# A decoder layer on one core: two of four weight sums of each Strassen unit by an adding transfer

## What is computed

```python
def _half_ffn(x, norm_g, w_gate, w_up, w_down):     # D_FF = 2816
    h = _rmsnorm(x, norm_g)
    return x + 0.5 * ((jax.nn.silu(h @ w_gate) * (h @ w_up)) @ w_down)
...
xp = _half_ffn(xp, ffn1_norm[l], ffn1_w_gate[l], ffn1_w_up[l], ffn1_w_down[l])
u, q, k, v = _project(_rmsnorm(xp, mix_norm[l]), pos_p, w_in[l], q_norm[l], k_norm[l])
mixed = jnp.concatenate([_pool_mix(u, pos_p, pool_w[l], pool_scale[l]),
                         _swa_prompt(q, k, v, attn_sinks[l])], axis=-1)
xp = xp + mixed @ w_out[l]
xp = _half_ffn(xp, ffn2_norm[l], ffn2_w_gate[l], ffn2_w_up[l], ffn2_w_down[l])
```

## Time and profile before

| | |
|---|---|
| median of 3 runs | 894.06 us (893.58 to 895.48) |
| profiled execution | 894.41 us, of which the span is 892.6 us |
| PE busy | 879.5 us (99%) |
| DVE busy | 659.2 us (74%) |
| ACT busy | 393.6 us (44%) |
| POOL busy | 32.4 us (4%) |
| DMA | 98.57 MB, mean 110 GB/s |

### The profile page before, as it was taken

One profiled execution on the slowest core, in us unless ns is written; L12 is line 12 of the kernel. 1 busy time (PEld: TensorE's weight loads), 2 busy tenths in 40 slices (PEclk: granted clock), 3 DMA queues, 4 the chain that ended last, 5 costly groups with the idle time before them and its releaser, 6 DMA issues.

```text
span 892.6 us, 17068 instructions
## 1 busy us (share of the span) xinstructions
PE 879.5 (99%) x7100; PEld 861.9 (97%) x7100; DVE 659.2 (74%) x956; ACT 393.6 (44%) x635; POOL 32.4 (4%) x37
## 2 busy tenths in 40 slices
PE   8999999999999999999988999999999999999998
PEld 7999999999999999999867999999999999999998
DVE  7969556997479976743777588997469984699844
ACT  8635213554135544433455446554125552255520
POOL 0000000000000000013322000000000000000000
PEclk9999999999999999999988999999999999999999
DMA  7233313422333323423201323433424424244241
GB/s 260 102 122 127 131 48 123 144 89 94 131 119 119 119 84 119 158 86 100 95 1 45 124 71 118 125 113 101 148 73 153 130 74 153 78 146 131 80 122 61
DMA packets 43180, 98.57 MB, mean 110 GB/s; under 512 B 4288, under 2 KB 5056, under 8 KB 43104
## 3 DMA queue, kind: packets, MB, share of 16 engines
q1 hardware_dynamic: 41056, 94.67, 32.0%
q10 hardware_dynamic: 2048, 2.81, 0.9%
HBM read 93.53 MB, written 3.60 MB: 109 GB/s over the span
## 4 chain that ended last, share of the span: by engine, by line
PE 93%; DVE 4%; ACT 1%; issue 1%; DMA 0%; POOLq 0%; SPq 0%; POOL 0%; DVEq 0%
PE ps L580 44%; PE ps L709 15%; PE ps L711 15%; PE ps L710 15%; PE ps L611 1%; ACT prob L1337 1%; DVE small L1832 1%; DVE prob L1848 1%; PE ps L768 1%; DMA raw<-gu 0%; DVE small L1836 0%; DVE wlo L1453 0%; PE ps L931 0%; PE ps L850 0%; PE ps L949 0%
## 5 line engine op out<-in xcount | busy, mean ns | idle before, releaser
L709 PE MATMUL ps<-xhi,whi 128*128 128x260 f32 (+1 forms) x1092 | 310.2, 284 | 0.1
L711 PE MATMUL ps<-xhi,wlo 128*128 128x260 f32 (+1 forms) x1092 | 310.0, 284 | 0.0
L710 PE MATMUL ps<-xlo,whi 128*128 128x260 f32 (+1 forms) x1092 | 309.6, 283 | 0.0
L709 PEld LDWEIGHTS ps<-xhi,whi 128*128 128x128 f32 x1092 | 205.4, 188 | 0.8 <-issue 0.6
L711 PEld LDWEIGHTS ps<-xhi,wlo 128*128 128x128 f32 x1092 | 205.5, 188 | 0.0
L710 PEld LDWEIGHTS ps<-xlo,whi 128*128 128x128 f32 x1092 | 205.4, 188 | 0.0
L1524 DVE TENSOR_TENSOR wlo<-full,whi 128x1024 fp32r<-128x1024 f32 (+1 forms) x117 | 160.3, 1394 | 0.0
L1065 ACT CAST whi<-raw 128x1024 fp32r<-128x1024 f32 (+1 forms) x75 | 75.3, 1004 | 178.3 <-PE ps L580 171.3
L580 PE MATMUL ps<-hhi,whi 128*128 128x268 f32 (+1 forms) x690 | 140.4, 285 | 0.3
L580 PE MATMUL ps<-hlo,whi 128*128 128x268 f32 (+1 forms) x690 | 140.1, 284 | 0.0
L580 PE MATMUL ps<-hhi,wlo 128*128 128x268 f32 (+1 forms) x690 | 139.7, 284 | 0.0
(11 more groups left out here) (194 smaller groups left out, 1082.6 us busy)
## 6 DMA issues: line engine op xcount, KB each, us to landing
full<-gu SPq DMA_DIRECT2D x78, 512.0 KB, 4.3
raw<-d SPq DMA_DIRECT2D x32, 448.0 KB, 3.5
full<-gu SPq DMA_DIRECT2D x39, 256.0 KB, 2.7
raw<-d SPq DMA_DIRECT2D x16, 512.0 KB, 3.6
raw<-w_in SPq DMA_DIRECT2D x10, 512.0 KB, 3.7
raw<-gu SPq DMA_DIRECT2D x9, 512.0 KB, 3.6
raw<-w_out SPq DMA_DIRECT2D x8, 512.0 KB, 4.5
xT<-x SPq DMA_DIRECT2D x8, 268.0 KB, 5.6
```

Source lines behind the costliest of these rows:

```text
L709: nc.tensor.matmul(dst, whi_t, xhi_t, start=(first and pr == 0), stop=False, skip_group_check=True)
L710: nc.tensor.matmul(dst, whi_t, xlo_t, start=False, stop=False, skip_group_check=True)
L711: last = nc.tensor.matmul(dst, wlo_t, xhi_t, start=False, stop=(pr == KC - 1), skip_group_check=True)
```

## The change

The first of VectorE's sums (line 1509) is taken out. In its place GpSimd issues a transfer for each unit that reads blocks 0 and 3 from memory once more (512 KB) and adds them to what stands in slots 1 and 4, after it has waited for the load of block 2 into these slots. `added` becomes one semaphore for each of the three buffers, counted up by 16 as the transfer lands; hi_a and the next sum wait for it. The transfers of stage 0 stand at the start of GpSimd's program, those of stage 1 at its end.

```diff
@@ build
-    added = sem("added")
+    added = [sem(f"added{r}") for r in range(3)]
@@ hi_a, on ScalarE
-            act.wait_ge(added, unit_no(s, p, i) + 1)
+            act.wait_ge(added[i % 3], k)
@@ weight_sums, on VectorE
             dve.wait_ge(b_loaded[r], k)
-            dve.wait_ge(c_loaded[r], k)
-            nc.vector.tensor_tensor(full[:, r, 1:5:3, :], full[:, r, 1:5:3, :], full[:, r, 0:7:6, :], ALU.add
-                                    ).then_inc(added, 1)
-            dve.wait_ge(added, u + 1)
+            dve.wait_ge(added[r], k)
@@ block.gpsimd, its start
+        def add_blocks(s, p, i):
+
+            f = AT[p] + i + (PLAIN[s] if p == 0 else 0)
+            r = i % 3
+            src = a[f"gu{s + 1}"][:, f * 4 * BLK:(f + 1) * 4 * BLK].rearrange("p (b c) -> p b c", b=4)
+            pool.wait_ge(c_loaded[r], 16 * (uses_before(s, p, i) + 1))
+            pool.dma_start(full[:, r, 1:5:3, :], src[:, 0:4:3, :], accum_op=ALU.add).then_inc(added[r], 16)
+
+        for p in range(3):
+            for i in range(PARTS[0][p]):
+                add_blocks(0, p, i)
         pool.wait_ge(unit_done, U_IN)
@@ block.gpsimd, its end
         pool_lo(3)
+
+        for p in range(3):
+            for i in range(PARTS[1][p]):
+                add_blocks(1, p, i)
```

## The result

| | before | changed |
|---|---|---|
| median | 893.54 us (892.21 to 895.88, 20 runs) | 898.48 us (894.23 to 903.6, 20 runs) |
| ratio | | 1.0052, 95% interval 1.0039 to 1.0065 |
| profiled execution, its span | 894.41 us, 892.6 us | 898.13 us, 896.3 us |
| standard deviation of the runs | 1.1 us | 2.3 us |

The changed kernel is 4.9 us slower by the medians and 3.7 us by the two profiled executions, and its runs lie twice as far apart.

What follows compares the result with a forecast made beforehand. TensorE, 93% of the span, was taken as the bound. Late adds at P5 cost 6.2 us, less 0.68 of existing stalls: 5.5 us on 894.41 gives 899.9 us profiled, 899.6 median; range 893.2 to 917.

Steps and rivals of the forecast that it cites:

- What bounds the kernel: Inside the units TensorE sets its own pitch, 0.123 us a matmul; removing the sums gains at most 0.68 us.
- rival (c): VectorE's relief is worth more than seen, 2 us or more, time 892 us or less; chance 0.04.
- The place and the mechanism: TensorE idles about 1 us at each part's first P5, five of six, keep_u2 behind hi_a behind the DMA.
- The slack table: Unit 1 of six parts: add's slack 6.43, 5.76, 5.67, 7.85, 6.08, 5.38 us; any excess delays P5 one for one.
- A: Time from block C's landing to the add's landing: taken as 7.1 us, floor 3.7, ceiling 10.0.
- GpSimd 0.9: GpSimd's waking and making of descriptors for the add, taken as 0.9 us, between 0.1 and 2.6.
- The addition, 1.3 us for a second read: The add reads memory and also the destination: 2.6 us of data, against 1.3 for a plain load.
- Rival (b): The adding itself is slow, over 10 us to landing; all six places lose, 928 us at 12; chance 0.19.
- Sharing with unit 2's loads: Unit 1's add runs half its data time beside unit 2's loads: 3.9 us of data instead of 2.6.
- The rule that was weighed: Skill page: GpSimd-issued transfer takes about 2.0 us plus bytes at 436 GB/s; the add would be hidden, gain 0.7 us.
- 10 us of cover: Unit 2: block C landed at 150.5, its hi_a runs at 160.64, so its add was costed at nothing.
- (a): The add is hidden, landing under 6.4 us after block C; time 893.4 to 895.9 us; chance 0.31.

Runs made afterwards that it cites:

- late add held back: Changed kernel with unit 1's add also waiting for blocks 0 and 1, and unit 2's loads held until P7 of unit 0: ratio 1.0172, 910.09 us.
- Unit 1 alone: Changed kernel with the adding transfer only for unit 1 of each part, VectorE's sum for the other 33 units: ratio 1.0038 to the kernel before.
- Two experiments that leaned on it: Changed kernel with unit 2's loads held until unit 1's add has landed, ratio 1.0236, or only until P7 of unit 0, ratio 1.0102.

## Why the prediction was right

**What bounds the kernel: right.** The claim that the matmuls' pitch owes nothing to VectorE was tested by leaving the sum out: 466 records in 57 us, and a gain of 0.13% (0.03 to 0.22%). The 2 us of rival (c) lie at the very end of that interval, and the pitch is unchanged, so (c) falls. That VectorE's busy time would fall by about 47 us took the sum of the instructions for busy time; it fell by 41.

**The place and the mechanism: right.** Forecast were gaps at P5 of unit 0 in five of six parts, at keep_u2 behind hi_a behind the DMA. The trace has them in four; in the second part of the earlier trace rows it is 1.67 us where 1.34 were forecast, in the others 0.74 (1.43), 0.61 (1.02), 1.09 (1.72), and none in the first, where 0.67 was forecast. Unit 1 alone carries the loss (1.0038), the other 33 units none (1.0000).

**The slack table: right.** Put in what the profile of the changed kernel shows from C's landing to the add's, 6.13, 7.18, 6.42, 6.17, 6.57 and 6.61 us, and the slacks of the prediction give 0, 1.42, 0.75, 0, 0.49 and 1.23, together 3.9 us (landings read to 0.1 us); measured 4.1. The late add held back gave 10.6 for 11.

**The size of A: near, in part by luck.** Forecast 7.1, measured 6.5 in the mean of the six; one term was too small and another too large.
- GpSimd 0.9: its plain transfer takes 0.4 to 0.5 us more than SyncE's, and 0.3 pass from C's landing to the issue. Together 0.7 to 0.8, about right.
- The addition, 1.3 us for a second read: measured 1.7. Rival (b), that the addition itself is slow, falls; whether the 1.7 are a second read isn't shown, only their size.
- Sharing with unit 2's loads, 1.3 us: the step that was mis-sized. I took the burst to cover half of the data time wherever it lay. In fact the cost is almost nothing with 1.4 us or more of lead in most cases, and 3 to 4 us with none. In the profiled execution it was 1.1 us at the place with 1.01 us of lead and 0.5 or less elsewhere, 0.4 in the mean.

**The total: 5.5 us forecast, 4.9 measured by the medians**, 3.7 in the two profiled executions. For the profiled execution the sum was 1.8 us too high, mostly by the sharing. These single executions differ from their medians: that of before was 0.9 us above its median over 20 runs. The changed kernel's next profile has only 2.3 us of P5 gaps. The sum was made for one execution, and what it priced varies from one to the next. That the runs would spread was not forecast. C's landing (3.5 to 4.6 us in the two profiles) sets both when the add starts and how much of the burst it meets, and with longer leads the deviation fell to 1.3 us. That this is the whole cause isn't shown: the late add held back, with undisturbed landings, has 2.1 us in five runs, and unit 1 alone 1.0 in five.

**The rule that was weighed.** The Trainium skill (DMA: Bandwidth & Descriptors, Anatomy of one DMA, SWDGE path) gave 3.2 us for a plain transfer, and 4.4 us as an estimate with the bytes counted twice; this case's runs have 4.1 and 5.8. By that rule the change would have been hidden. The measurement decides: the plain figure was short by 0.9 us, and the estimate by 1.4 us for an adding transfer. Counting the bytes twice was my step and not the page's, which gives no time for an adding transfer.

**What was wrong in the prediction and cost nothing there:** "10 us of cover" for unit 2 left out the add's own 6.5 us. It also left out that unit 2's own block C would land after 6.2 us instead of 3.5. Two experiments that leaned on it missed. Two figures beside the sum were added up wrong: the cost at A = 6.4 is 32.0 - 29.3 - 0.68 = 2.0 us, not 1.8, and the full gain of (a) ends at 893.4, not at the 893.2 of the range. Neither changes a conclusion.

## What to carry to other kernels

Work taken from an engine that the bound engine does not wait for brought nothing here, though that engine was 90% busy; and the transfer that replaced it brought a latency into a chain that had had room for the sum but not for it. Find the one instance with the least time from its input to its deadline (here the first buffer that is free only at the end of a stage), because the other 33 of 39 say nothing about it. And price a transfer by when it is issued against the next burst, not by its bytes alone: the same 512 KB took from 5.6 to 10.1 us.

## What the runs showed of the hardware that was not expected

- An adding transfer and a burst of three loads (1.25 MB in all) issued close to it don't share evenly; in the runs the one issued first was delayed little, and the other was by some 2 to 3 us. With the add issued up to 0.7 us behind the load of block C, or up to 0.6 us ahead of it, unit 1's add took 8.2 to 9.0 us and that load 3.6 to 4.3. With the add 1.0 to 2.2 us ahead, it took mostly 5.8 to 6.9 us and the load 5.1 to 6.7. With 2.9 us and more both were mostly as if alone. Three pairs were late on both sides (7.9 and 7.2 us at 0.84, 7.6 and 7.1 at 1.73, 6.6 and 6.3 at 3.3). It looks like service in the order of arrival; the runs don't show which part of a transfer waits.
- After some idle gaps in the FFNs TensorE comes back at half clock: after each of the five of 4.6 us and more, and after seven of 1.94 to 3.2 us, the granted clock was 0.50 to 0.69 over the next 4 us (0.50 is the lower level, 1.2 GHz), and a tail costs about 2 us more. After gaps of 1.88 us and less the clock stayed at 1.00; and so it did after some longer ones, up to one of 3.5 us. The first two rows follow gaps of 1.94 and 2.66 us in the kernel with the late add held back, the last two are the gap of 3.5 us and what follows it in the kernel with the adding transfer for unit 1 alone:
```profile
156.30:160.30 4.00, 4.00 (x23) 4.00 (x24) 3.21 (x6) 2.81 (x4) 1.20 (x1) 0.69 0.75 166
275.00:279.00 4.00, 4.00 (x34) 4.00 (x34) 3.20 (x6) 2.81 (x5) 1.00 (x1) 1.00 0.83 162
...
784.70:787.90 3.20, 0.00 (x0) 0.00 (x0) 1.34 (x3) 1.43 (x3) 0.00 (x0) 1.00 0.83 269
788.00:792.00 4.00, 4.00 (x34) 4.00 (x35) 3.21 (x5) 2.83 (x5) 0.00 (x0) 1.00 0.28 69
```
  Length of the gap alone does not decide.
